# A mixer and FFN layer on one core: the shift of the first modulation is added late, and eight tiles of the conditioning product are summed after the recurrence

## The reference, cut to what matters

```
mod = silu(c) @ w_ada + b_ada                  # 6 parts of 1024: sh1, sc1, gt1, sh2, sc2, gt2
h   = rms_norm(x, g_pre_mix) * (1 + sc1) + sh1
zin = h @ w_in                                 # cv_val, cv_gate, q, f, i, og
out_a = silu(layer_norm(causal_conv31(cv_val * sigmoid(cv_gate))))
out_b = hgrn2(q, f, i, og)                     # gated recurrence, 4 heads
x  = x + gt1 * rms_norm([out_a, out_b] @ w_out, g_post_mix)
h2 = rms_norm(x, g_pre_ffn) * (1 + sc2) + sh2
gate, up = split(h2 @ w_ffn_in)
out = x + gt2 * rms_norm((silu(gate) * up) @ w_ffn_out, g_post_ffn)
```

## Time and profile before

| | |
|---|---|
| median of 3 runs | 1121.51 us |
| the profiled execution | 1123.33 us, of it 1120.8 us span |
| PE, DVE, POOL, ACT busy | 96%, 74%, 70%, 45% of the span |
| granted TensorE clock | 0.997 of full speed |

### The profile page before, as it was taken

The page is one execution under the profiler, slowest core; times in us unless marked ns, Lnnn a source line. Parts: engine busy times, 40 slices in busy tenths (PEclk is TensorE's granted clock), DMA queues, the critical chain, the costliest instruction groups (busy, mean ns, idle before and its releaser), DMA issues.

```text
span 1120.8 us, 14373 instructions
## 1 busy us (share of the span) xinstructions
PE 1079.6 (96%) x5043; PEld 893.3 (80%) x5043; DVE 826.1 (74%) x1155; ACT 501.9 (45%) x853; POOL 779.6 (70%) x673
## 2 busy tenths in 40 slices
PE   2899999999999999999999999999999999999996
PEld 1678888888877888888888888888888888888885
DVE  5987997979998745678775767676666666666658
ACT  5755565574652834345333333233333333333334
POOL 7658967667773630427977777778686869696966
PEclk9999999999999999999999999999999999999998
DMA  9624324232321271212222222222221212212217
GB/s 344 223 79 146 104 85 125 83 115 72 96 75 39 76 250 69 94 39 85 83 71 62 70 63 75 67 70 72 60 74 59 79 60 70 72 60 73 67 51 295
DMA packets 98744, 108.00 MB, mean 96 GB/s; under 512 B 6541, under 2 KB 76402, under 8 KB 98674
## 3 DMA queue, kind: packets, MB, share of 16 engines
q1 hardware_dynamic: 97216, 102.79, 28.8%
q10 hardware_dynamic: 1458, 4.31, 1.0%
HBM read 98.68 MB, written 8.40 MB: 96 GB/s over the span
## 4 chain that ended last, share of the span: by engine, by line
PE 83%; DVE 6%; ACT 2%; issue 2%; POOL 1%; DMA 1%; DVEq 0%; ACTq 0%
PE pair L2180 34%; PE pair L2200 17%; PE pair L1989 16%; PE pair L2089 8%; PE pair L2143 2%; PE pair L2223 2%; PE pair L2022 1%; DVE qk L1544 1%; DVE tt L1537 1%; DMA ada<-in_w_ada 1%; DVE pair L1507 1%; DVE qk L1551 1%; POOL ada L746 1%; DVE pmat L1560 1%; PE pair L2017 1%
## 5 line engine op out<-in xcount | busy, mean ns | idle before, releaser
L1808 DVE TENSOR_TENSOR yt<-yt,pair 128x512 f32<-128x512 f32 x264 | 176.1, 683 | 35.3 <-PE pair L2200 35.3
L746 POOL TENSOR_TENSOR ada<-ada,cond 128x256 f32<-128x256 f32 x128 | 101.8, 828 | 64.2 <-DMA ada<-in_w_ada 64.0
L844 POOL TENSOR_TENSOR raw_r<-raw,w_hi 128x512 fp32r<-128x512 f32 x68 | 96.2, 1415 | 65.0 <-ACT w_hi L1263 65.0
L1507 DVE SCALAR_TENSOR_TENSOR pair<-u,conv_w_col,pair 128x512 f32<-128x512 f32 x208 | 139.6, 746 | 1.9 <-ACT pair L1127 1.4
L2200 PE MATMUL pair<-w_lo,op_hi 128*128 128x512 f32 x280 | 109.1, 389 | 0.0
L2200 PE MATMUL pair<-w_hi,op_lo 128*128 128x512 f32 x280 | 109.0, 389 | 0.0
L2200 PE MATMUL pair<-w_hi,op_hi 128*128 128x512 f32 x280 | 108.9, 389 | 0.0
L853 POOL TENSOR_TENSOR w_lo<-w_lo_f,w_hi 128x512 fp32r<-128x512 f32 x70 | 95.3, 1362 | 0.0
L2180 PE MATMUL pair<-t_lo,w_hi 128*128 128x512 f32 x240 | 93.7, 390 | 0.0
L2180 PE MATMUL pair<-t_hi,w_hi 128*128 128x512 f32 x240 | 93.4, 389 | 0.0
L1263 ACT ACTIVATE w_hi<-raw 128x512 fp32r<-128x512 f32 x68 | 42.6, 626 | 73.0 <-PE pair L2180 71.8
(11 more groups left out here) (327 smaller groups left out, 3007.8 us busy)
## 6 DMA issues: line engine op xcount, KB each, us to landing
ada<-in_w_ada SPq DMA_DIRECT2D x48, 512.0 KB, 4.8
raw<-in_w_ffn_in SPq DMA_DIRECT2D x56, 256.0 KB, 2.9
raw<-in_w_in SPq DMA_DIRECT2D x24, 512.0 KB, 5.5
w_lo_f<-in_w_ffn_out SPq DMA_DIRECT2D x40, 256.0 KB, 3.0
w_hi_f<-in_w_ffn_out SPq DMA_DIRECT2D x30, 256.0 KB, 3.1
x<-in_x SPq DMA_DIRECT2D x8, 512.0 KB, 8.0
raw<-in_w_out SPq DMA_DIRECT2D x8, 512.0 KB, 3.4
x<-in_x SPq DMA_DIRECT2D x4, 1024.0 KB, 8.8
```

The source lines that it names most:

```text
L746: i_ = pool.tensor_tensor(ada[:, n % ADA_RING, cols], ada[:, n % ADA_RING, cols], cond[:, cols], ALU.mult)
L844: pool.tensor_tensor(place_part(at), place_full(at), place_part(GU_HIGH[m % 3]), ALU.subtract).then_inc(gu_low, 1)
L1507: i_ = dve.scalar_tensor_tensor(out=dst, in0=tap_of(j + 1, h), scalar=tap_weight(j + 1, t), in1=dst, op0=ALU.mult, op1=ALU.add)
L1808: i_ = dve.tensor_tensor(dst, dst, bank(4 + t), ALU.add)
```

## The change

- The prologue makes normed x times scale only, without the shift, and keeps it in the place of x (`first_tile`). The 8 scales are loaded and summed ahead, the 8 shifts behind them, all 16 on DVE (`scale`, `shift`). The halves are taken in another order: five channel tiles of the first four token tiles, then the same of the last four, then the rest. PE turns four groups before the first projection.
- The first three chunks of w_in (gate, val, i) are multiplied with the tokens without shift. Their weights are loaded into a place of their own in halves (`load_first`, `split_first`). What the shift would add is one number a column: DVE sums weight times shift over the channel tiles (`first_biases`), three one-column matmuls sum over partitions (`first_columns`), and the sum is added where the chunks are read out (sigmoid bias, `gated_first`, bias of vt). Chunk i goes into the fourth PSUM pair, at once after the groups (`project_first`).
- For all later chunks the tokens are split again with the shift: `shifted_high` on ACT, `shifted_low` on DVE, 8 instructions of 128x1024 each, each after `project_first` has used that channel tile. Chunk 3 waits for them tile by tile. POOL's loop starts after the last of them.
- `TAPS_FIRST` goes from 42, 35, 35, 42 to 30, 34, 35, 42.
- The ring in the mixer carries 24 tiles of w_ada, not 32 (2, 1, 2, 1 behind the chunks). The last eight (gt2) are loaded by SP: four once the last period's slots allow, four behind the x loads of the output projection. DVE sums them after the last `mix_low` and ahead of `residual(0)`. The second gain is stored near the end.

```diff
-TAPS_FIRST = [42, 35, 35, 42]
+TAPS_FIRST = [30, 34, 35, 42]
-GROUPS = [(kt, half) for kt in range(KT) for half in range(2)]
+GROUPS = ([(kt, half) for half in range(2) for kt in range(5)] + [(kt, half) for kt in range(5, KT) for half in range(2)])
 # SP, its order written short
+            load_scale(0); load_scale(1); load_x(0..3); load_first(0, 0); load_first(1, 0)
+            load_scale(2..5); load_x(4..7); load_first(0, 1); load_first(1, 1)
+            load_scale(6); load_scale(7); load_first(2, 0); load_first(2, 1)
+            load_shift(0..7); load_chunk(WS); load_chunk(WS + 1)
 ...
+            sp.wait_ge(tap_done, HEADS * TAP_STEPS)
+            for n in range(ADA_LATE):
+                load_late(n)
             for g in range(N_IN + WS, N_IN + N_OUT):
                 load_chunk(g)
             sp.wait_ge(mix_lo, N_OUT)
             for i in range(4):
                 sp.dma_start(x1[:, 2 * i:2 * i + 2, :], x_d[:, 2 * i:2 * i + 2, :]).then_inc(x1_loaded[i], 16)
+            for n in range(ADA_LATE, KT):
+                load_late(n)
 # ACT
+            high(WS)
+            for kt in range(2):
+                shifted_high(kt)
             evacuate(0)
-            high(WS)
+            for kt in range(2, KT):
+                shifted_high(kt)
 # DVE
+            for g in range(8, 16):
+                low_half(g)
+                shift(g - 8)
+            first_biases()
+            shifted_low(0)
+            shifted_low(1)
+            dve.memset(u[:, 0:TAPS - 1], 0.0)
+            dve.wait_ge(bias_made, 1)
+            dve.tensor_copy(first_bias[:, :], bank(4)[:, 0:WS]).then_inc(bias_ready, 1)
+            shifted_low(2)
+            shifted_low(3)
             lower_bounds()
+            gated_first()
+            for kt in range(4, KT):
+                shifted_low(kt)
+            def first_biases():
+                dve.tensor_tensor(mod[:, 0:KT], sums0[:, 1, :], vec[:, ROW_BADA:ROW_BADA + KT], ALU.add).then_inc(shift_ready, 1)
+                for kt in range(KT):        # 128x384 each
+                    me.done(dve.scalar_tensor_tensor(out=dst, in0=src, scalar=mod[:, kt:kt + 1], in1=dst, op0=ALU.mult, op1=ALU.add))
+                dve.tensor_tensor(bias_sum[:, 0, :, :], bias_sum[:, 0, :, :], bias_sum[:, 1, :, :], ALU.add).then_inc(bias_summed, 1)
+            def late_tile(n):
+                dve.wait_ge(late_loaded[n % ADA_LATE], 16 * (n // ADA_LATE + 1))
+                dve.scalar_tensor_tensor(out=src, in0=src, scalar=1.0, in1=cond[:, :], op0=ALU.mult, op1=ALU.mult,
+                                         accum_out=mod[:, 5 * KT + n:5 * KT + n + 1]).then_inc(late_summed, 1)
+            for n in range(KT):
+                late_tile(n)
+            late_gain()
             for i in range(TT):
                 residual(i)
 # PE
+            def project_first():
+                pe.wait_ge(w_split, WS)
+                for kt in range(KT):
+                    split_product(pair[3], 2, ...).then_inc(first_used if kt < KT - 1 else w_used, 1)
+                    if kt == 4:
+                        first_columns()
 ...
+                    if g == WS:
+                        pe.wait_ge(again_ready, kt + 1)
```

More of the change, by code:

```diff
@@ L163, in ada_rows @@
     t, c = divmod(g - 1, 5) if g > 5 else (0, g - 2)
-    return [KT * t + 2 * c, KT * t + 2 * c + 1] if t < 4 and 0 <= c < 4 else []
+    if t >= 4 or not 0 <= c < 4:
+        return []
+    first = ADA_ROWS // 4 * t + (0, 2, 3, 5)[c]
+    return list(range(first, first + (2, 1, 2, 1)[c]))
 def slots_at(period, piece):
@@ L321, in build @@
         ada_summed = sem("ada_summed")
+        late_loaded = [sem(f"late_loaded{i}") for i in range(ADA_LATE)]
+        late_summed = sem("late_summed")
         ring_free = sem("ring_free")
@@ L567, in _, with load_scale @@
[L567 to L577, removed]
+            def load_scale(kt):
+                sp.dma_start(ada0[:, kt, :], w_ada_d[:, KT + kt, :]).then_inc(scale_loaded[kt], 16)
@@ new lines, in load_x @@
+            def load_x(i):
+                sp.dma_start(x0[:, i, :], x_d[:, i, :]).then_inc(x_loaded[i], 16)
+            sp.dma_start(cond[:, :], t_in["c"].to_broadcast([P, D])).then_inc(c_loaded, 16)
+            load_scale(0)
+            load_scale(1)
+            for i in range(4):
+                load_x(i)
+            load_first(0, 0)
+            load_first(1, 0)
+            for kt in range(2, 6):
+                load_scale(kt)
+            for i in range(4, TT):
+                load_x(i)
@@ L993, in full_and_high @@
                 act.wait_ge(mod0_ready, kt + 1)
[L994 to L997, removed]
+                act.activation(first_tile(kt, half), turns_of(group_bank(g)), ACT.Copy, scale=gs[:, 0, kt:kt + 1]
+                               ).then_inc(full0_ready, 1)
                 act.wait_ge(full0_ready, g + 1)
@@ L1017, in _, with shifted_high @@
-            act.wait_ge(vec_ready, 3)
+                act.activation(turns_of(dst), first_tile(kt, half), ACT.Copy).then_inc(hi_ready, 1)
+            def shifted_high(kt):
+                act.wait_ge(shift_ready, 1)
+                if kt < KT - 1:
+                    act.wait_ge(first_used, kt + 1)
+                else:
+                    act.wait_ge(w_used, WS)
+                dst = (ha_hi if kt < 4 else hb_hi)[:, kt % 4, :]
+                act.activation(turns_of(dst), x0[:, :, kt * P:(kt + 1) * P], ACT.Identity, bias=mod[:, kt:kt + 1]
+                               ).then_inc(again_hi, 1)
@@ L1019, in high @@
+            squares(range(4))
+            for g in range(3):
+                full_and_high(g)
+            squares(range(4, 6))
+            full_and_high(3)
+            squares(range(6, TT))
+            for g in range(4, 16):
+                full_and_high(g)
+            act.wait_ge(vec_ready, 2)
+            act.activation(lb_tmp[:, 1, :], lb_tmp[:, 0, :], ACT.Exp).then_inc(cond_ready, 1)
+            act.preload_act_table_set("sigmoid_and_others")
             def high(g):
-                act.wait_ge(raw_loaded[g % RAW], 16 * (g // RAW + 1))
+                act.wait_ge(raw_loaded[g % RAW], raw_count(g))
```

334 lines of the change are left out of this document (215 added, 119 removed).

## The result

The changed kernel takes 1130.98 us (median of 18 runs, 1129.23 to 1132.61) against 1122.07 of the kernel before (18 runs, one at 1133.96, the others 1120.98 to 1124.49): ratio 1.0071, 95% interval 1.0056 to 1.0085. It is slower, and by more than was forecast (1124.7).

The account below looks back on a forecast made before the run. PE, 96% busy, was taken as the bound. Front and mixer -7.3, tail stall +8.7 and low clock +1.8 gave +3.2 us: 1124.7 against the median of 1121.51, with 1116 to 1130 for 8 in 10.

Parts of the forecast that it names:

- Start of chunk 3: Prologue: DVE's list lets chunk 3 start at 66.9 in place of 75.97, 9.1 us gained.
- It ends tile 3's normalising at 16.2 as before: Prologue, DVE: normalising of token tile 3 ends at 16.2, unchanged by the change.
- the 0.9 for scale 2: Prologue, DVE's list up to the last low part: 0.9 us added for scale 2.
- 2 for POOL's splits: Prologue, DVE's list up to the last low part: 2 us added for POOL's splits.
- PE waits 4.1 us: Between project_first and chunk 3: PE idles 4.1 us until gated_first is done at 66.9.
- The clock in front: Prologue stall: may cost PE the same clock loss, but counted 0 because DVE is what is late there.
- Period 1: Mixer's first period: DVE is filled and stalls PE by 2.9 us, bounds 0 and 6.
- Relief from eight tiles fewer, less one tap in period 2: Mixer: POOL multiplying 24 tiles, not 32, gives 1.6 us, mostly in the last period; one more tap lowers it.
- Tail stall: Output projection: late tiles 4 to 7 land behind x, delay residual(0), stall PE 8.7 us before tile 4.
- Low clock in the tail: Output projection behind the stall: PE returns at half clock and loses 1.8 us, bounds 0 and 3.
- Second gain, late loads, biases on PE: Gain's way through DRAM hidden, late loads in a quiet stretch, one-column matmuls 0.1 each: no cost in the sum.
- Rival 4: Prologue and period 1: second split and POOL's late start lose the front's gain; 1130.0 us, chance 0.12.

Follow-up runs that it names:

- e9: e8 with other_vectors on DVE moved behind group 1's low part and PE's two transposes behind its first four turn_x; 1115.36 us, ratio 0.9937.
- e8: e2 with gated_first made right behind shifted_low 1 and the bias copy, ACT's shifted_high 2 and 3 ahead of its sigmoid; 1114.7 us, ratio 0.9933.
- e7: e2 with 17 unused 128x512 matmuls added on PE between project_first and chunk 3; 1118.6 us, ratio 0.9967.
- e5: The kernel before with only the change's tail: 24 tiles in the ring, eight late tiles ahead of residual(0); 1130.98 us, ratio 1.0078.
- e4: The changed kernel with its tail half undone: 32 tiles in the ring, no late tiles, both gains stored together; 1124.98 us, ratio 1.0022.
- e6: The kernel before with only the change's tail, four late tiles ahead of residual(0), one behind each of residual 0 to 3; 1118.86 us, ratio 0.9968.
- e2: The changed kernel with late tiles 4 to 7 moved one by one behind residual 0 to 3; 1119.61 us, ratio 0.9968.
- e10: The changed kernel with 36 unused 128x512 matmuls added on PE ahead of token tile 4; 1128.32 us, ratio 1.0058.
- e1: The changed kernel with other_vectors behind the four normalise_x on DVE and PE's two transposes behind its first four turn_x; 1131.16 us, ratio 1.0076.

## Why the prediction was wrong

It had the shape of the change right, a gain in front, a stall in period 1, a larger stall in the output projection, and the sign. The first of its terms was mis-sized by more than all the others together leave, so that +3.2 became +7.7. Its range of 1116 to 1130 ends below the measured 1130.98. Term by term, predicted and then measured between the two profiled executions:

- **Start of chunk 3: -9.1, then -3.7.** This is the step that failed: the time of DVE's list up to chunk 3. Its first fault is the sentence "It ends tile 3's normalising at 16.2 as before". The changed kernel has `other_vectors` ahead of `normalise_x(0)`, and PE's transposes ahead of `turn_x(0)`; both wait for the last of nine loads. The forecast counted the instructions on DVE and not the waits that they carry with them: 3.66 late. From there to the last low part the list took 35.0 in place of 34.0, and from that to chunk 3 17.4 in place of 16.7; the ten instructions of the biases took 6.8 in place of 5.7. The six products take 5.08; at the shortest one's 605 ns they would take 3.6, so some 1.5 are lost beside POOL's split from 57.09 to 60.88, where 1.2 were counted. 5.4 in all.
- **The same list without the wait.** The wait is not the whole fault. e9 has none: it ends tile 3 at 16.27 and has the last low part out at 53.5, where the forecast has 50.2. So the list itself was 3.3 too short, and in the changed kernel the wait hid most of that: taking it away gave 1.3 at the last low part and 1.4 at period 1's query level. The terms in question are the 0.9 for scale 2, "2 for POOL's splits" and the copies of the vectors, which had no term; how the 3.3 divide between them isn't shown.
- **The chain behind the biases.** "PE waits 4.1 us" was measured as 4.15: right. It was taken as given, and e8 shows that it was an order that could be changed.
- **The clock in front: 0, then 1.7 on PE by 98.** PE idled 4.15 us, came back at 1.00, and had a clock of 0.50 from 73 to 76. The reason given for 0, "DVE is what is late there", holds in part: by e7 some 0.7 of the 1.7 are waited for at the query level anyway, and some 1.0 come through. Lead and low clock can't be added up without that wait.
- **Period 1: +2.9, then +1.24,** within its bounds; the DIAG slot was not late on DVE, which even idled 1.27 us ahead of it. With the earlier chunk 3 that was forecast more of the wait comes out: e8, whose chunk 3 starts near 68, has 0.62, 0.79 and 0.57 ahead of the 1.20, 3.2 in all. Its lead of some 8 us at chunk 3 is 3.9 at the query level (127.51 against 131.44), 4.1 lost on the way where the forecast took 2.9.
- **Relief from eight tiles fewer, less one tap in period 2: -1.1, then -3.4** (the lead grows from 0.6 to 4.0 between 131 and 418), inside the bound of 4. It is not "mostly in the last" period's idle time: e5 has no wait from 76 to 328, and e4 shows that a full DVE needs this relief in period 1 too. e6 against before puts it at 3.5 by the times.
- **Tail stall: +8.7, then +9.8.** Right place, right cause, right size: e2 removes it with one reordering. The 1.1 above the forecast appear at late tile 6, for which DVE waited another 1.42 us. The second four are issued over 5.95 us, each behind the sum that frees its buffer, but the queue moved 397 GB/s or more in every window from 398 to 411, so whether the late issue or the queue's other traffic cost it isn't shown. Tiles 0 and 1 took 3.42 and 3.40 us instead of 1.22, beside POOL's `wo_lo`; DVE then still waited 5.00 us for tile 4. The Trainium skill (SBUF — State Buffer, section SBUF: two separate sides) calls the shared port an exclusive lock between DVE and GpSimd; these two rows agree with it. The six products above lost only 1.5 us beside four POOL quarters of 3.79 in all, so DVE isn't shut out for the whole of such a stretch.
- **Low clock in the tail: +1.8, then +1.4** by e10. Right.
- **Second gain, late loads, biases on PE: 0, then 0.** The store at 1080.7 and load at 1096.8 of the gain are hidden. 0.5 us between 440 and the end and 0.2 in period 1 are not explained.

Rival 4 had named the front as lost, with "DVE has no gap to recover in from 60 to 125", and its time, 1130.0, is the nearest of all. It had 0.12 of the chances. By e4 and e5 it was the better description of the front: with 32 tiles the front costs 2.6 us, with 24 it is worth nothing. Its price in the tail (8.7 and 1.8) was the forecast's own.

## What to carry to other kernels

When a step is moved ahead in an engine's program, write down what each of its instructions waits for, and add that wait to everything behind it; counting durations alone gave 9.1 us where 3.7 came. Then look at what stands close behind that wait: without it only 1.4 of 3.5 us came through. Where two engines pass work to and fro, a lead of one ends at the next place where it waits for the other: look for the order in which the other makes its results (e8: some 4 us without one instruction less). Work that is put off must be interleaved at the place where it lands, one piece behind each step of the urgent chain, not as a block ahead of it: the same eight tiles cost 9.8 us of PE's time as a block and nothing measurable between the residuals.

## What the runs showed of the hardware

- The granted clock doesn't fall at a fixed point of PE's idle time. In the tail it fell some 2.4 us after PE stopped at 418.64 (1.00 in the window 420 to 421, 0.54 in 421 to 422), and PE came back at 0.50. In front PE stopped at 68.14, and the clock was 1.00 through all 4.15 us of idle time and fell only behind the restart at 72.29:

```profile
71.00:72.00 1.00, 0.00 (x0) 0.00 (x0) 1.00 (x2) 1.00 (x2) 0.00 (x0) 1.00 0.00 0
72.00:73.00 1.00, 0.71 (x3) 0.65 (x4) 1.00 (x2) 1.00 (x2) 0.00 (x0) 0.96 0.00 0
73.00:74.00 1.00, 1.00 (x3) 0.73 (x3) 1.00 (x2) 1.00 (x2) 0.00 (x0) 0.50 0.06 16
```

- It rose some time after PE was busy again: 0.83 in the window 76 to 77, some 4 us behind the restart; in e1, where it had fallen before the restart (0.58 in 71 to 72), after nearly 6; in the tail after 2.9. The Trainium skill (TensorE: Matmul & The Clock Gate, Part 1) says that idleness lowers and activity restores the clock; both are shown here, and matmuls of no use kept it at 1.00 in e7 and e10.
- The load of `rows_b`, 62 KB issued at 5.07 while the core's DMA engines moved 296 to 418 GB/s, released its waiters 9.11 us later. Nine loads of 0.5 to 62 KB share that semaphore, so which of them was the last to land isn't shown.
